# One decoder step, eight sequences of cached attention: the latent pages read a second time in 32-word pieces, transposed in blocks by VectorE, and 15 of 31 convolution taps put on GpSimd

## The chip, the core and the metric

The kernel runs on one core of a Trainium2 chip. The metric is the device time of one execution in microseconds. The kernel before took 1145.48 us (median of 3 runs, 1144.85 to 1145.82).

## The reference

One layer of a hybrid decoder, in float32, for two groups with the same weights: a prompt of 256 tokens and 8 sequences that decode one token each, against 2048 cached positions. A feed-forward half step, one projection, latent attention beside a causal depthwise convolution, a gated merge, and a second feed-forward half step. The two parts that the change touches:

```python
def absorb(carry, kv_blk, kr_blk, mask):                 # one page of 128 cached tokens of each sequence
    m, l, acc = carry
    k = _mla_keys(kv_blk, kr_blk, w_uk, g_k_head)        # kv_blk (128, 256) @ w_uk (256, 16*64), rope part, norm over 96
    sc = jnp.einsum('bshd,bphd->bhsp', qf, k) * scale
    ...
    acc = acc * corr[..., None] + jnp.einsum('bhsp,bpl->bhsl', p, kv_blk)
...
buf = jnp.concatenate([buf_prev, z], axis=1)             # 30 earlier rows, then z
y = conv(buf, w_dw) + b_dw                               # 31 taps per channel, 1024 channels
```

`cache_kv_latent` is (160, 128, 256) and `page_table` names the 16 pages of each sequence.

## The kernel before

All engines run hand-written programs that meet in semaphores. TensorE multiplies in float32r with each operand split in a high and a low part: `product` issues three matmuls (high x high, high x low, low x high; lines 1894 to 1896). The middle of the kernel goes through the 8 sequences, 16 pages of 128 tokens each, sequence 0 by itself, 1 to 6 in a loop and 7 at the end.

For each page, in four steps that overlap with those of the pages beside it:

- **TensorE, `turn`** (L2329): the page lies in `kv2` with the token on the partition. Two matmuls against the identity (L2342, L2343) turn it to latent-by-token into the PSUM bank 0. Every fourth page the rope rows of four pages are turned too (L2336), and a page later they are multiplied with the rope queries (L2338).
- **ScalarE, `page_hi`** (L1026) copies the turned page from PSUM to `kTH`, rounded; **VectorE, `page_lo`** (L1609) subtracts that from PSUM and leaves the rest in `kTL`.
- **TensorE, `keys`** (L2345): 18 matmuls of 320 to 384 columns against `wqH` and `wqL` give the page's keys of all heads and the scores of its sequence.
- **ScalarE, `page_sq`** copies the scores (L1035) and squares the keys (L1038); **VectorE, `page_sum`** sums the squares by head (L1614).

`kTH` and `kTL` hold two pages each, so the split of page n + 1 is made while TensorE computes page n. Between these, VectorE does the softmax of the sequence before in small steps (`norm_sums`, `inverse_norms`, `scores` with the maximum at L1673, `subtract`, `sums`) and the convolution: one block of 128 channels in a sequence, 31 taps on 128x256 (L1699 to L1703), spread over the pages by the table `TAPS`. GpSimd takes the maximum over the partitions (L676), squares the rope rows (L674), makes the convolution of the sample rows (L647 to L655) and adds up the blocks (L665). Behind page 10 (`VALUES_PAGE`) TensorE multiplies the probabilities of the sequence before with its 16 pages (L2367); each quarter releases four pages of `kv2`.

SyncE's queue issues the loads. For a page it reads the page number from `table` (L418), then issues the page (L425, 128 rows of 1 KB) and its rope rows (L428, 128 rows of 128 bytes). `kv2` holds two sequences; the loads of sequence b wait for the values of sequence b - 2 (`pg_rel`, L418 in the profile). Sequences 0 and 1 are loaded ahead, while the prompt's attention runs.

Of the kernel before, what the change touches and what calls it, by code (L numbers as in the profile page):

```python
# [83 lines left out]
VALUES_PAGE = 10  # L84
TAPS = (0, 1, 1, 0, 2, 2, 1, 2, 2, 2, 7, 3, 2, 3, 1, 2)
TAPS_FIRST = (2, 3, 3, 0, 2, 3, 0, 3, 3, 0, 3, 3, 0, 2, 2, 2)
# [52 lines left out]
def decoder_layer(nc, x, out):  # L139
    ctx = ExitStack()  # L140
    with ctx:
# [27 lines left out]
        vecT = sb("vecT", [P, V_N])  # L169
        gbc = sb("gbc", [P, B_N])  # L170
# [5 lines left out]
        ztmp = sb("ztmp", [P, NB, CW - 1], at=base[0] - 2112)  # L176
# [20 lines left out]
        wuvF = sb("wuvF", [P, 2, D], at=W + 16896)  # L197
        yH = sb("yH", [P, KT, T], F32R, at=W)
# [157 lines left out]
        kv2_in = [sem(f"kv2_in{g}") for g in range(8)]  # L356
        qx_done, den_ps, mx_done, gmx_done, sub_done, p_done, lsum_done = map(
# [12 lines left out]
        six_ps, six_res = sem("six_ps"), sem("six_res")  # L370
        own_act, own_dve, own_pool = sem("own_act"), sem("own_dve"), sem("own_pool")
# [18 lines left out]
        def _(sp):  # L390
# [29 lines left out]
            def page_group(i, s, g):  # L420
                b = 2 * i + s
# [10 lines left out]
            def sample_pages(i, s):  # L432
                for g in range(4):
                    sp.wait_ge(pg_rel, 4 * (2 * i + s) + g + 1)
                    page_group(i, s, g)

            def first_pages(s, groups):

                for g in groups:
                    sp.wait_ge(sc_ps, 4 * g + 4)  # L440
                    page_group(0, s, g)
# [175 lines left out]
        def _(pool):  # L617
# [40 lines left out]
            def conv_sum(f_):  # L658

                pool.wait_ge(tap_done, f_ + 1)  # L660
                if f_ == 0:
# [5 lines left out]
            pool.wait_ge(st_sb, 4)  # L667
            sample_rows(0)
            for b in range(NB):
                pool.wait_ge(kTH_done, NPG * b + 14)  # L670
                if b >= 1:
                    pool.wait_ge(norm_sum, b)
                kr = kr2[:, b % 2, :, :]
                nc.gpsimd.tensor_tensor(krq[:, :, :], kr, kr, ALU.mult).then_inc(kr_sq, 1)  # L674
                pool.wait_ge(mx_done, b + 1)
                nc.gpsimd.partition_all_reduce(gmx[:, b % 2, :], mx[:, b % 2, :], P, bass.bass_isa.ReduceOp.max  # L676
                                               ).then_inc(gmx_done, 1)
                pool.wait_ge(p_done, b + 3)
                nc.gpsimd.tensor_copy(snew[:, b, :], Pr[0:NB, b % 2, NPG, H * (b % 2):H * (b % 2) + H]).then_inc(prn_done, 1)
                if b < NB - 1:  # L680
                    conv_sum(b)
                    sample_rows(b + 1)
            conv_sum(NB - 1)
# [22 lines left out]
        def _(act):  # L706
# [314 lines left out]
            def page_hi(pg, n):  # L1021
                act.wait_ge(kT_ps, pg + 1)
                act.wait_ge(kn_ps, pg + 1)
                if n % 4 == 0:
                    f(krT[:, (n // 4) % 2, :], PS[:, 0, KL:KL + P], ACT.Copy)
                f(kTH[:, n % 2, :], PS[:, 0, 0:KL], ACT.Copy).then_inc(kTH_done, 1)  # L1026
# [25 lines left out]
            def sequence(b, s, first=False, last=False):  # L1052
                for n in range(NPG):
                    pg = NPG * b + n
                    if not (last and n == NPG - 1):
                        page_hi(pg + 1, (n + 1) % NPG)
# [10 lines left out]
            page_hi(0, 0)  # L1067
# [94 lines left out]
        def _(dve):  # L1162
# [436 lines left out]
            def page_lo(pg, n, b, s, first):  # L1599
# [3 lines left out]
                if n % 4 == 1:  # L1603
                    own.wait()
# [4 lines left out]
                v.tensor_tensor(kTL[:, n % 2, :], PS[:, 0, 0:KL], kTH[:, n % 2, :].bitcast(F32), ALU.subtract  # L1609
                                ).then_inc(kTL_done, 1)  # L1610
# [27 lines left out]
            page_lo(0, 0, 0, 0, True)  # L1638
# [895 lines left out]
```

## Time and profile before

| | |
|---|---|
| runs, us | 1145.82, 1144.85, 1145.48 (median 1145.48) |
| profiled execution, us | 1145.37, of it span 1143.5 |
| TensorE clock granted, mean | 0.997 |
| busy: TensorE, VectorE, ScalarE, GpSimd | 98%, 68%, 51%, 6% |
| DMA, mean over the span | 149 GB/s |

The span runs from the first to the last instruction of the profiled execution; the 1.9 us that its time is longer lie outside. Matmuls are pipelined, so that a busy TensorE is one that always has a matmul in its array; what a matmul costs is the distance from its start to the next one's. The mean busy shares hide the stages: the pages of the sequences lie between about 400 and 815 us of the span.

### The profile page before, as it was taken

To read this page: it belongs to the slowest core of one execution; us is meant where nothing else is said; L and a number is where in the kernel's file an instruction comes from. 1 tells how busy PE (TensorE), PEld (TensorE's weight loads), DVE (VectorE), ACT (ScalarE), POOL (GpSimd) and SP (SyncE) were. 2 spreads that over 40 slices of the span, in tenths; PEclk is the share of its full clock that TensorE was granted. 3 is DMA by queue.
4 is the path that set the end of the run, shared out by engine and by line. 5 is a ranking of instruction groups with operands and counts; after the bars stand their busy time and mean duration, and the time that the engine had idled before them with its cause. 6 is when DMAs were issued, how large, how long until landed. Compare 5 with 4: busy or idle time off the path is not lost.

```text
span 1143.5 us, 25908 instructions
## 1 busy us (share of the span) xinstructions
PE 1122.7 (98%) x9549; PEld 1086.8 (95%) x9549; DVE 778.4 (68%) x1325; ACT 581.7 (51%) x1153; POOL 67.8 (6%) x136
## 2 busy tenths in 40 slices
PE   5999999999999999999999999999999999999998
PEld 3899999999898899999999999999999999999998
DVE  4655553567777688888888888888757666555543
ACT  3444453346576655455545454554566545444432
POOL 2000000010000100101010110101020010000000
PEclk9999999999999999999999999999999999999999
DMA  9987578947344440021211202032257684555552
GB/s 324 314 292 269 183 254 289 348 167 222 99 142 127 133 133 2 20 65 33 52 47 36 62 22 73 13 84 71 57 150 254 227 272 131 183 183 177 177 184 71
DMA packets 165629, 169.84 MB, mean 149 GB/s; under 512 B 25780, under 2 KB 144071, under 8 KB 165525
## 3 DMA queue, kind: packets, MB, share of 16 engines
q1 hardware_dynamic: 163799, 166.83, 45.6%
q10 hardware_dynamic: 1742, 1.88, 0.5%
q8 instruction: 50, 0.82, 0.3%
q14 instruction: 38, 0.31, 0.1%
HBM read 167.13 MB, written 2.49 MB: 148 GB/s over the span
## 4 chain that ended last, share of the span: by engine, by line
PE 92%; DVE 2%; SPq 2%; ACT 1%; DMA 1%; issue 1%; POOL 0%; DVEq 0%; ACTq 0%
PE PS L1894 27%; PE PS L1895 27%; PE PS L1896 27%; PE PS L1971 2%; SPq L451 2%; PE PS L2367 1%; PE PS L2342 1%; PE PS L2343 1%; DMA raw<-in_w_ffn_in 1%; PE PS L2288 1%; PE PS L2099 1%; PE PS L2308 0%; PE PS L2338 0%; DVE wL L1172 0%; PE PS L2287 0%
## 5 line engine op out<-in xcount | busy, mean ns | idle before, releaser
L1172 DVE TENSOR_TENSOR wL<-raw,wH 128x1024 fp32r<-128x1024 f32 (+2 forms) x208 | 246.3, 1191 | 209.8 <-ACT wH L717 208.4
L717 ACT ACTIVATE wH<-raw 128x1024 fp32r<-128x1024 f32 (+2 forms) x208 | 213.2, 1029 | 245.6 <-PE PS L1896 224.7
L1894 PE MATMUL PS<-uH,wH 128*128 128x264 f32 x1024 | 294.2, 287 | 4.5 <-DVE uL L1233 4.0
L1895 PE MATMUL PS<-uL,wH 128*128 128x264 f32 x1024 | 291.8, 285 | 0.0
L1896 PE MATMUL PS<-uH,wL 128*128 128x264 f32 x1024 | 291.4, 285 | 0.0
L1894 PE MATMUL PS<-wqH,kTH 128*128 128x336 f32 (+2 forms) x768 | 255.7, 333 | 0.0
L1896 PE MATMUL PS<-wqH,kTL 128*128 128x336 f32 (+2 forms) x768 | 246.1, 320 | 0.0
L1895 PE MATMUL PS<-wqL,kTH 128*128 128x336 f32 (+2 forms) x768 | 245.9, 320 | 0.0
L1894 PEld LDWEIGHTS PS<-uH,wH 128*128 128x128 f32 x1024 | 193.9, 189 | 7.9 <-issue 6.4
L1895 PEld LDWEIGHTS PS<-uL,wH 128*128 128x128 f32 x1024 | 194.2, 190 | 0.0
L1896 PEld LDWEIGHTS PS<-uH,wL 128*128 128x128 f32 x1024 | 193.6, 189 | 0.0
L1614 DVE TENSOR_REDUCE nsum<-sqb 128x16 f32<-128x1024 f32 x128 | 155.0, 1211 | 1.1 <-ACT sqb L1038 1.1
L1895 PEld LDWEIGHTS PS<-wqL,kTH 128*128 128x128 f32 x768 | 144.6, 188 | 0.0
L1894 PEld LDWEIGHTS PS<-wqH,kTH 128*128 128x128 f32 x768 | 144.4, 188 | 0.0
L1896 PEld LDWEIGHTS PS<-wqH,kTL 128*128 128x128 f32 x768 | 144.2, 188 | 0.0
L1038 ACT ACTIVATE sqb<-PS 128x640 f32<-128x640 f32 (+1 forms) x256 | 138.6, 599 | 0.0
L1035 ACT ACTIVATE S<-PS 128x16 f32<-128x16 f32 x128 | 23.2, 182 | 192.0 <-PE PS L1896 192.0
L1701 DVE SCALAR_TENSOR_TENSOR u<-zbuf,wdw,u (+1 forms) x232 | 113.9, 491 | 8.2 <-DVE u L1701 7.6
L1894 PE MATMUL PS<-aH,wH 128*128 128x264 f32 x352 | 100.6, 286 | 0.0
L1895 PE MATMUL PS<-aL,wH 128*128 128x264 f32 x352 | 100.2, 285 | 0.0
L1896 PE MATMUL PS<-aH,wL 128*128 128x264 f32 x352 | 99.9, 284 | 0.0
L1609 DVE TENSOR_TENSOR kTL<-PS,kTH 128x256 fp32r<-128x256 f32 x128 | 53.8, 421 | 42.4 <-ACT kTH L1026 41.9
(343 smaller groups left out, 1497.8 us busy)
## 6 DMA issues: line engine op xcount, KB each, us to landing
raw<-in_w_ffn_in SPq DMA_DIRECT2D x86, 512.0 KB, 3.5
adaw<-in_w_ada SPq DMA_DIRECT2D x72, 512.0 KB, 6.5
raw<-in_w_ffn_out SPq DMA_DIRECT2D x32, 512.0 KB, 3.5
raw<-in_w_in SPq DMA_DIRECT2D x32, 512.0 KB, 4.5
kv<-in_cache_kv_latent SPq DMA_DIRECT2D x128, 128.0 KB, 2.0
raw<-in_w_ffn_out SPq DMA_DIRECT2D x16, 384.0 KB, 3.0
raw<-in_w_attn_out SPq DMA_DIRECT2D x8, 512.0 KB, 4.1
raw<-in_w_conv_out SPq DMA_DIRECT2D x8, 512.0 KB, 4.7
```

The lines of the kernel that those rows point to most:

```text
L451: sp.dma_start(adaw[slot][:, 2 * c:2 * c + 2, :], ada_v[:, 2 * c:2 * c + 2, ADA_W * j:ADA_W * j + ADA_W]).then_inc(ada_in[2 * slot + c // ...
L717: f(wH[:, k, 0:width], raw[:, k, 0:width], ACT.Copy).then_inc(w_hi, 1)
L1035: f(S[:, s, n, :], PS[:, b0 + bank, c:c + H], ACT.Copy)
L1038: i_ = f(sqb[:, n % 2, at:at + (k1 - k0) * w].rearrange("p (k w) -> p k w", w=w), PS[:, b0 + k0:b0 + k1, c:c + w], ACT.Square)
L1172: v.tensor_tensor(wL[:, k, 0:width], raw[:, k, 0:width], wH[:, k, 0:width].bitcast(F32), ALU.subtract).then_inc(w_lo, 1)
L1609: v.tensor_tensor(kTL[:, n % 2, :], PS[:, 0, 0:KL], kTH[:, n % 2, :].bitcast(F32), ALU.subtract).then_inc(kTL_done, 1)
L1614: v.tensor_reduce(nsum[:, s, n, :], sqb[:, n % 2, :].rearrange("p (h d) -> p h d", h=H), AX_X, ALU.add).then_inc(knsum_done, 1)
L1701: own.done(v.scalar_tensor_tensor(out=y, in0=z, scalar=w, in1=y, op0=ALU.mult, op1=ALU.add))
L1894: mm(dst, a[0], b[0], start=start, stop=False)
L1895: mm(dst, a[0], b[1], start=False, stop=False)
L1896: return mm(dst, a[1], b[0], start=False, stop=stop)
L1971: i_ = mm(PS[QUAD * g:QUAD * g + NS, bank, 0:P], csil[:, kt, :], w[:, g, :, :], start=(kt == 0), stop=(kt == KT - 1))
```

## The change

Pages of sequences 1 to 7 are no longer turned by TensorE. Each is read from HBM a second time, into a new buffer `kx` of eight pages, in an order in which a transposition of 32x32 blocks gives the page with the latent word on the partition. VectorE does that transposition (`page_turn`, one instruction of 128x256 a page, two pages ahead), from `kx` to `kT32`. ScalarE and VectorE then split the page out of `kT32`, in SBUF, through the view `BLOCKS` that puts the tokens in their order. Sequence 0 is turned as before. The loads of sequences 1 to 7 are written out in place of a loop, groups of four `kx` pages between groups of `kv2` pages.

GpSimd takes 15 of the 31 taps, each as a product (into `yp` or `ytmp`) and, but for the first, an addition; VectorE keeps 16. The maximum over partitions, the copy of the new probabilities and the squares of the rope rows stand between parts of these taps in GpSimd's program. The values of the sequence before come behind page 8 in place of 10.

```diff
-VALUES_PAGE = 10
-TAPS = (0, 1, 1, 0, 2, 2, 1, 2, 2, 2, 7, 3, 2, 3, 1, 2)
+VALUES_PAGE = 8
+TAPS = (0, 0, 0, 0, 1, 1, 0, 1, 3, 1, 1, 2, 2, 2, 1, 1)
+DVE_TAPS = sum(TAPS)
+POOL_TAPS = (DVE_TAPS, DVE_TAPS + 5, DVE_TAPS + 9, DVE_TAPS + 12, CW)
...
+        kx = sb("kx", [P, 8, KL], at=W + 16896)
+        kT32 = sb("kT32", [P, 2, KL], at=gains)
...
+        BLOCKS = [kT32[:, e, :].rearrange("p (k h t) -> p h t k", k=4, h=2) for e in range(2)]
...
+            def block_group(b, g):
+                for k in range(4):
+                    pg = page(NPG * b + 4 * g + k)
+                    src = x["cache_kv_latent"][ds(pg, 1), :, :].rearrange(
+                        "o (t k) (h q i) -> q (o t k h) i", t=QUAD, q=4, i=QUAD)
+                    sp.dma_start(kx[:, 4 * (g % 2) + k, :], src
+                                 ).then_inc(kx_in[g % 2], 16)
+            def blocks_next(b, g):
+                sp.wait_ge(kx_ps, NPG * b + 4 * g - 20)
+                block_group(b, g)
+            def pages_next(b, s, g):
+                sp.wait_ge(pg_rel, 4 * b + g + 1)
+                page_group(b, s, g)
+            def sequence_loads(b):
+                s = b % 2
+                blocks_next(b, 2)
+                blocks_next(b, 3)
+                pages_next(b + 1, 1 - s, 0)
+                blocks_next(b + 1, 0)
+                pages_next(b + 1, 1 - s, 1)
+                blocks_next(b + 1, 1)
+                pages_next(b + 1, 1 - s, 2)
+                pages_next(b + 1, 1 - s, 3)
...
+            block_group(1, 0)
+            block_group(1, 1)
+            for b in range(1, NB - 1):
+                sequence_loads(b)
+            blocks_next(NB - 1, 2)
+            blocks_next(NB - 1, 3)
+            sp.wait_ge(kx_ps, PAGES - NPG)
             sp.dma_start(wuvF[:, :, :], uv).then_inc(in_wuv, 16)
-            with sp.Fori(1, 4) as i:
-                sample_pages(i, 0)
-                sample_pages(i, 1)
...
+            def taps(f_, part):
+                for t in range(POOL_TAPS[part], POOL_TAPS[part + 1]):
+                    z, w = zbuf[:, f_, t:t + SEQ], wdw[:, f_, t:t + 1].to_broadcast([P, SEQ])
+                    own.wait()
+                    if t == DVE_TAPS:
+                        own.done(g.tensor_tensor(yp[:, :], z, w, ALU.mult))
+                    else:
+                        own.done(g.tensor_tensor(ytmp[:, :], z, w, ALU.mult))
+                        own.wait()
+                        own.done(g.tensor_tensor(yp[:, :], yp[:, :], ytmp[:, :], ALU.add))
...
+            def page_turn(b, n):
+                if n % 4 == 0:
+                    dve.wait_ge(kx_in[n // 4 % 2], 128 * b + 64 * (n // 8) - 64)
+                dve.wait_ge(kTL_done, NPG * b + n + 1)
+                v.transpose(kT32[:, n % 2, :], kx[:, n % 8, :]).then_inc(kx_ps, 1)
...
+                    v.tensor_tensor(lo_.rearrange("p (h t k) -> p h t k", h=2, k=4), BLOCKS[n % 2],
+                                    hi_.rearrange("p (h t k) -> p h t k", h=2, k=4), ALU.subtract
+                                    ).then_inc(kTL_done, 1)
...
+                if turned:
+                    tr(PS[:, 0, 0:128], kv2[:, NPG * s + n, 0:128], ident)
+                    tr(PS[:, 0, 128:256], kv2[:, NPG * s + n, 128:256], ident).then_inc(kT_ps, 1)
```

How the order moves, at two places. First SyncE's queue in the loads of a sequence (`table` holds the page numbers, `kv_...` and `kr_...` are `kv2` and `kr2`). Before, one page in the loop:

```order
L418 ISA
L418 TENSOR_LOAD table
L418 ISA x2
L425 ISA
L425 DMA kv_122<-in_cache_kv_latent 128x256
L428 ISA
L428 DMA kr_110<-in_cache_k_rope 128x32
```

Now, where a group of `kx` pages ends and one of `kv2` pages begins:

```order
L429 TENSOR_LOAD table
L429 ISA x2
L448 ISA
L448 DMA kx<-in_cache_kv_latent 128x8x32
L429 TENSOR_LOAD table
L429 ISA x2
L435 ISA
L435 DMA kv_126<-in_cache_kv_latent 128x256
L438 ISA
L438 DMA kr_114<-in_cache_k_rope 128x32
```

Every page of sequences 1 to 7 has gained a read of the table and a transfer whose rows are cut into 8 pieces of 32 words, in the one queue that also brings the pages and the rope rows.

Second VectorE, at the third page of a sequence in the loop. Before:

```order
L1609 TENSOR_TENSOR kTL<-PS,kTH 128x256
L129 REGISTER_ALU
L1701 ISA
L1701 SCALAR_TENSOR_TENSOR u<-zbuf,wdw,u 128x256
L1614 TENSOR_REDUCE nsum<-sqb 128x16
L1666 RECIPROCAL nsum<-nsum 128x128
```

Now (`kT_86` is `kT32`):

```order
L1691 STREAM_TRANSPOSE kT_86<-kx 128x256
L1708 TENSOR_TENSOR kTL<-kT_86,kTH 128x256
L1714 TENSOR_REDUCE nsum<-sqb 128x16
L1766 RECIPROCAL nsum<-nsum 128x128
```

The transposition of the page after next stands ahead of the subtraction of the next page, and the subtraction reads two tensors in SBUF; the tap is gone from this page.

## Rows read from the trace of the kernel before

**Rows 1.** The page: busy time by engine; tenths busy in 40 slices; granted clock.

```profile
PE 1122.7 (98%) x9549; PEld 1086.8 (95%) x9549; DVE 778.4 (68%) x1325; ACT 581.7 (51%) x1153; POOL 67.8 (6%) x136
...
PE   5999999999999999999999999999999999999998
PEclk9999999999999999999999999999999999999999
```

**Rows 2.** Chain that ended last, 456.4 to 771.2 us: shares by line.

```profile
by line: PE PS L1896 27.8%; PE PS L1895 27.7%; PE PS L1894 27.7%; PE PS L2367 3.6%; PE PS L2342 3.5%; PE PS L2343 3.2%; issue 2.0%; PE PS L2338 1.2%; PE PS L2336 1.0%; ACT sqb L1038 0.5%; DVE kTL L1609 0.3%; DVE olrow L1690 0.3%; DVE u L170
```

**Rows 3.** VectorE's timeline: start us, us, line, op; score maximum of two sequences.

```profile
456.37 0.64 DVE L1673 TENSOR_REDUCE mx<-S 128x16 f32<-128x272 f32 x1
...
771.17 0.64 DVE L1673 TENSOR_REDUCE mx<-S 128x16 f32<-128x272 f32 x1
```

**Rows 4.** Busy us of PE, PEld, DVE, ACT, POOL; PEclk; DMA share; GB/s.

```profile
456.40:771.20 314.80, 314.45 (x2198) 305.51 (x2197) 263.20 (x484) 162.81 (x433) 32.15 (x72) 1.00 0.17 46
```

**Rows 5.** VectorE by line, same stretch: count, busy us, mean ns, idle.

```profile
L1701 DVE SCALAR_TENSOR_TENSOR u<-zbuf,wdw,u x174 | 85.2, 490 | 7.6 <-DVE u L1701 7.6
L1609 DVE TENSOR_TENSOR kTL<-PS,kTH 128x256 fp32r<-128x256 f32 x96 | 40.4, 421 | 26.8 <-ACT kTH L1026 26.5
```

**Rows 6.** VectorE's block transposition: count, min/median/max ns.

```profile
L1240 DVE STREAM_TRANSPOSE modt<-PS x18: 307/310/319, 22.3 to 950.3; 128x128 f32<-128x128 f32 x18
```

**Rows 7.** Timeline of VectorE, then of GpSimd, at the same moments.

```profile
526.03 0.48 DVE L1701 SCALAR_TENSOR_TENSOR u<-zbuf,wdw,u  x1
526.42 1.21 DVE L1614 TENSOR_REDUCE nsum<-sqb 128x16 f32<-128x1024 f32 x1
...
527.55 0.62 DVE L1701 SCALAR_TENSOR_TENSOR u<-zbuf,wdw,u  x1
...
525.44 0.75 POOL L665 TENSOR_TENSOR ysum<-ysum,u 128x264 f32<-128x264 f32 x1 [7.45 <-issue]
...
527.45 1.81 POOL L653 TENSOR_TENSOR ztmp<-ztmp 128x120 f32<-128x120 f32 x5
```

**Rows 8.** One line each, min/median/max ns: GpSimd additions of 128x264; VectorE's taps.

```profile
L625 POOL TENSOR_TENSOR u<-u x15: 738/747/1704, 10.6 to 931.5; 128x264 f32<-128x264 f32 x15
...
L1701 DVE SCALAR_TENSOR_TENSOR u<-zbuf,wdw,u x232: 465/477/1004, 395.1 to 808.3; - x87, 128x256 f32<-128x256 f32 x29
```

**Rows 9.** SyncE's queue, timeline: start us, us, line, transfer.

```profile
554.57 0.34 SPq L425 DMA_DIRECT2D kv<-in_cache_kv_latent  x1
555.09 0.33 SPq L428 DMA_DIRECT2D kr<-in_cache_k_rope  x1
556.25 0.34 SPq L425 DMA_DIRECT2D kv<-in_cache_kv_latent  x1
```

**Rows 10.** SyncE's waits, same stretch: us in total, times, longest.

```profile
SPq L418 <- PE PS L2367: 175.2, 6, 54.3
```

**Rows 11.** DMA, 657.51 to 658.76 us: one page's rope rows.

```profile
DMA packets 145, 0.02 MB, mean 13 GB/s; under 512 B 145, under 2 KB 145, under 8 KB 145
## 3 DMA queue, kind: packets, MB, share of 16 engines
q1 hardware_dynamic: 145, 0.02, 8.7%
```

**Rows 12.** DMA, 456.4 to 771.2 us, the same columns.

```profile
q1 hardware_dynamic: 27671, 14.19, 16.9%
```

**Rows 13.** DMA, 102.4 to 107.5 us: tenths busy and GB/s in 40 slices.

```profile
DMA  9999000000000000630999255555555540022149
GB/s 835 2574 514 498 0 0 0 0 0 0 0 0 0 0 0 0 32 24 8 466 1405 1887 88 177 193 193 193 193 193 193 193 193 145 8 0 8 8 16 121 305
```

**Rows 14.** SyncE's queue at the start, 8 issues merged; then the whole line.

```profile
2.70 6.14 SPq L451 DMA_DIRECT2D adaw<-in_w_ada  x8
...
L451 SPq DMA_DIRECT2D adaw<-in_w_ada x72: 367/507/2492, 2.7 to 917.0; - x72
```

**Rows 15.** DMA, 0 to 8.84 us: packets, MB, share.

```profile
q1 hardware_dynamic: 872, 2.02, 67.6%
```

More of the change, by code:

```diff
@@ L356, in decoder_layer @@
         kv2_in = [sem(f"kv2_in{g}") for g in range(8)]
+        kx_ps, kr_ps = sem("kx_ps"), sem("kr_ps")
+        kx_in = [sem(f"kx_in{g}") for g in range(2)]
         qx_done, den_ps, mx_done, gmx_done, sub_done, p_done, lsum_done = map(
@@ L660, in conv_sum @@
                 pool.wait_ge(tap_done, f_ + 1)
+                own.wait()
+                own.done(g.tensor_tensor(u[:, f_, 0:SEQ], u[:, f_, 0:SEQ], yp[:, :], ALU.add))
+                own.wait()
                 if f_ == 0:
@@ L677, in _, with new_probabilities @@
                                                ).then_inc(gmx_done, 1)
+            def new_probabilities(b):
                 pool.wait_ge(p_done, b + 3)
-                nc.gpsimd.tensor_copy(snew[:, b, :], Pr[0:NB, b % 2, NPG, H * (b % 2):H * (b % 2) + H]).then_inc(prn_done, 1)
+                nc.gpsimd.tensor_copy(snew[:, b, :], Pr[0:NB, b % 2, NPG, H * (b % 2):H * (b % 2) + H]
+                                      ).then_inc(prn_done, 1)
+            pool.wait_ge(st_sb, 4)
+            sample_rows(0)
+            for b in range(NB):
+                taps(b, 0)
+                if b >= 1:
+                    score_max(b - 1)
+                taps(b, 1)
+                if b >= 1:
+                    new_probabilities(b - 1)
+                taps(b, 2)
+                rope_square(b)
+                taps(b, 3)
                 if b < NB - 1:
@@ L682, in _ @@
                     sample_rows(b + 1)
+            score_max(NB - 1)
+            new_probabilities(NB - 1)
             conv_sum(NB - 1)
@@ L1054, in sequence @@
                     pg = NPG * b + n
-                    if not (last and n == NPG - 1):
-                        page_hi(pg + 1, (n + 1) % NPG)
+                    if n + 1 < NPG:
+                        page_hi(b, n + 1, first)
+                    elif not last:
+                        page_hi(b + 1, 0)
                     if n == 1 and not first:
@@ L1709, in sequence @@
                     pg = NPG * b + n
+                    if n + 2 < NPG:
+                        if not first:
+                            page_turn(b, n + 2)
+                    elif not last:
+                        page_turn(b + 1, n + 2 - NPG)
                     if not (last and n == NPG - 1):
-                        page_lo(pg + 1, (n + 1) % NPG, b, s, first)
+                        page_lo(pg + 1, (n + 1) % NPG, b, s, first, first and n + 1 < NPG)
                     taps = (TAPS_FIRST if first else TAPS)[n]
@@ L1749, in _ @@
             with dve.Fori(0, 3) as i:
-                own.loop(i, 2 * (CW + 10))
+                own.loop(i, 2 * (DVE_TAPS + 10))
                 sequence(2 * i + 1, 1)
@@ L2327, in denominator, with turn @@
                 mm(PS[:, 0, 448:448 + H], ones[:, :], lsum[:, s, :], start=True, stop=True).then_inc(den_ps, 1)
-            def turn(use, s, n, pg, b, first):
+            def turn(use, s, n, pg, b, first, turned=False):
                 if n % 4 == 0:
@@ L2375, in sequence @@
                     if n + 1 < NPG:
-                        turn(use, s, n + 1, pg + 1, b, first)
+                        turn(use, s, n + 1, pg + 1, b, first, first)
                     elif not last:
@@ L2403, in _ @@
                     pe.wait_ge(masked, H)
-                    turn(0, 0, 0, 0, 0, True)
+                    turn(0, 0, 0, 0, 0, True, True)
             values(H - 1)
```

62 lines of the change are left out of this document (36 added, 26 removed).

## Prediction

> **What bounds the kernel now.** I read the page first: TensorE is busy in 98% of the span, at 9 tenths in every slice but the first and the last, with the granted clock at its 2.4 GHz level [rows 1]. So time can only be gained where TensorE has less to do, and lost wherever something makes it wait. Then the stretch that the change touches. The maximum of the scores comes once in a sequence, and from the first to the seventh 314.80 us pass [rows 3]: 52.47 us a sequence, 3.28 us a page. In it TensorE is busy for 314.45 us and VectorE for 263.20, GpSimd for 32.15 [rows 4]. The chain of waits says the same by line: the key matmuls have 83%, and the two transpositions that the change takes away have 3.5% and 3.2% [rows 2]. Last I read the SyncE queue and the DMA, which are no bound today: the queue waits 175.2 us of the stretch for pages to be released [rows 10], and its transfers take 16.9% of the 16 engines [rows 12].
>
> **TensorE: removed.** 6.7% of 314.80 us is 21.1 us for 96 pages, 0.220 us a page. The change removes it for 112 pages: 24.6 us. If all else keeps pace, a sequence falls from 52.47 to 48.95 us, a page to 3.06. The added semaphore increments and the move of the values from page 10 to 8 cost TensorE nothing: its work is the same, only two pages earlier.
>
> **VectorE: hidden.** It goes from 31 taps to 16 in a sequence. A tap lasts 0.490 us [rows 5], but overlaps its successor; 526.03 to 526.42, where the next operation starts, is some 0.40, so 15 taps are 6.0 us, and the 7.6 us of waits between dependent taps [rows 5], 1.3 a sequence, mostly go with the row of seven. A transposition of 128x128 takes 0.310 us [rows 6]; the 128 further columns can cost nothing (lower end) or the same again (0.62, upper end). I take 0.44, 0.36 after overlap, near the 0.421 of the subtraction with the same 256 columns [rows 5]: 5.8 us for 16. VectorE's 43.9 busy us (263.20 / 6) so end at 43 to 44, under 48.95. The subtraction of the low part now reads two SBUF tensors in place of PSUM and SBUF; I price it as before, at 0.42, and ScalarE's copy too.
>
> **GpSimd: hidden, if its operations leave VectorE alone.** 29 operations on 128x256; the nearest row is 0.75 us for 128x264 [rows 7], so 21.8 us, beside 5.4 that it has (32.15 / 6). It fits in 48.95, at the upper end too if not every operation takes the 1.70 us maximum [rows 8]. The cover is thin; see the third rival.
>
> **SyncE and the DMA: here I put the loss.** A `kx` page is 128 KB in 1024 pieces of 128 bytes. The rope rows are such pieces: in a window with one page's 128 pieces and 17 semaphore writes, 145 packets take 8.7% of 16 engines in 1.25 us, 1.74 us or 12.0 ns each [rows 11]. What decides is on how many engines the 1024 pieces go. When the queue copies the conv state of the samples (line 415), 8 rows in 16 pieces of 59 KB, the pieces start in two turns, slices 1 to 4 and 20 to 22 (a piece is counted whole in the slice where it starts), and behind the second turn a weight load gets a steady 193 GB/s at 5 tenths, half of the engines [rows 13]: 8 rows were dealt to 8 engines, though there were 16 pieces. The source of a `kx` page has 4 outer rows (the `q` of the rearranged pattern), the destination 128; if the deal goes by what divides both, the page goes on 4 engines, 256 pieces each: 256 x 12.0 = 3.07 us a page. The Trainium skill, DMA: Bandwidth & Descriptors, section "Why a DMA increments its semaphore by 16 and not by 1", says so outright: the engines used are the largest number up to 16 that divides the slowest dimension of both patterns, which here is 4. The trace agrees for 8 rows; no transfer in it has different outer dimensions on its two sides.
>
> Those four engines carry their share of the pages too: 16.9% of 314.80 us is 53.2 us per engine for 96 pages, 0.55 us a page. Worse, the queue is held. At the start of the kernel the eighth load in a row is out only at 8.84 us, and a single issue lasts up to 2.49 us where the median is 0.51 [rows 14]. By 8.84 us about 2450 pieces were issued (8 x 256 of these loads, 400 before) and 872 had begun [rows 15]: an estimate of 100 pieces per engine is what fits ahead. A `kx` transfer has 256 on each of its four, so SyncE stands on it until 156 are gone, and what is behind it in the queue, the table read, the pages and rope rows of the next sequence, stands too. For such a page SyncE needs 1.68 us (554.57 to 556.25) [rows 9], while the four engines need 0.55 of that.
>
> The sum for one round of `sequence_loads` (16 `kx` pages, 16 pages): 16 x 3.07 = 49.2, and 16 x 1.68 = 26.9, less what still runs on the engines when the queue changes from `kx` to pages, three times 100 x 12.0 ns = 3.6: 72.5 us, against 48.95 of TensorE. VectorE waits in `page_turn`, TensorE behind it for `kTL`. Six rounds are 435.0; the last eight `kx` pages 24.6. Ahead of the first round some 4.5 us of sequence 1 pass (its first eight pages are loaded in sequence 0, and the first buffer is free at its second page), and behind the last group 2 us to land and four pages at 3.06: 14. Together 478 us from the start of sequence 1 to the end of 7, where 7 x 52.47 = 367 are spent now. That is +111 us. The profiled execution has 1145.37 us (span 1143.5 and 1.9 around it), 0.1 under the median: I forecast **1256 us**. The weights that are loaded behind the pages come no later relative to their use than by two pages, and I give them nothing.
>
> Bounds of this case: if the queue can run ahead without limit, a page costs the four engines 3.07 + 0.55 = 3.62 us, a round 57.9, the whole 391: +23, 1169 us. If a piece that is one of eight in a strided row takes 16 ns in place of 12 (a third more; no row shows it), the round is 65.6 + 26.9 - 4.8 = 87.7, the whole 577: +210, 1355 us.
>
> **Rivals.**
> - *All 16 engines carry `kx`* (the deal goes by the 128 rows of the destination). Then a page costs 0.77 us of each engine, SyncE 1.16 us (an issue and the table read, 555.09 to 556.25 [rows 9]) beside 1.68: 2.84 us a page against 3.06. It just fits, and the 24.6 us are gained: **1121 us**. For it: nothing in the trace contradicts; a row of 128 partitions always used all engines. Against it: rows 13.
> - *16 engines, and GpSimd in VectorE's way.* A tap beside GpSimd's additions lasts 0.62 us in place of 0.48 [rows 7], one 1.00 us, and an addition up to 1.70 in place of 0.75 [rows 8]. VectorE now has 32 operations a sequence with two SBUF inputs, and GpSimd is busy 27 us of 49: each meets it with 0.56 and waits half an operation, 0.21 us, 6.7 us a sequence. VectorE comes to 51, above TensorE: seven sequences give back 7 x 2 = 14 us: **1135 us**. The Trainium skill, SBUF — State Buffer, section "Who interferes with whom", has VectorE's second read port shared with GpSimd, whoever is first keeping it for the whole instruction; the lengthened rows agree. It speaks against this change, most for the subtraction, whose second SBUF input is new.
> - *The pieces are covered after all*: four engines, but 9 ns or less a piece and no holding; the round is about TensorE's own time, and the gain of 24.6 us is eaten by late groups: within 0.2% of before.
>
> **How the numbers follow.** Four engines and a loss: 0.70. Sixteen engines: 0.25, of it 0.14 clean and 0.11 with VectorE in the way. Covered: 0.05. A measurement of this kernel can tell about 0.2%, 2.3 us, from no change. So faster 0.25, same 0.05, slower 0.70. The likeliest case alone has 1169 to 1355. The range for 8 in 10 must reach into the faster cases, which hold more than 2 in 10: 1121 to 1310, leaving out the dearest pieces and a little below.
>
> **What would show it.** Right: VectorE's transposition of every fourth page waits several us for `kx`; the issues of `kx` last 2 us or more each; DMA stands near 2 or 3 tenths and never above in the stretch; two score maxima are some 72 us apart; TensorE's busy share in the stretch is about two thirds, its clock possibly lower in the gaps. Wrong: issues of 0.35 to 0.5 us and a full DMA burst of under 1 us a page would mean 16 engines; then two maxima 49 us apart give the first rival, 51 us with taps of 0.6 us and more the second. If the issues are short but VectorE still waits for `kx`, the holding was wrong and the lower bound holds.

## The result and the profile after

The changed kernel takes 1252.91 us, the median of 4 runs (1250.25 to 1255.57), where the kernel before has 1145.58 in the same comparison: a ratio of 1.0938, 95% interval 1.0912 to 1.0964. The profiled execution, the longest of the four, has 1255.57 us with a span of 1253.7. Line numbers from here on are those of the changed kernel: the table read is L429, the page's transfer L435, its rope rows L438, the `kx` transfer L448, the block transposition L1691, the subtraction `kTL` L1708, ScalarE's copy `kTH` L1110, a tap L1801.

First the score maxima in VectorE's timeline (start us, us, line, op), beside [rows 3]:

```profile
584.86 0.62 DVE L1773 TENSOR_REDUCE mx<-S 128x16 f32<-128x272 f32 x1
...
655.83 0.63 DVE L1773 TENSOR_REDUCE mx<-S 128x16 f32<-128x272 f32 x1
...
726.91 0.62 DVE L1773 TENSOR_REDUCE mx<-S 128x16 f32<-128x272 f32 x1
```

They are 70.97 and 71.08 us apart, where [rows 3] give 52.47 a sequence. From the first maximum to the last (of sequence 7) 468.3 us pass, against 359.9 before: that is 108.4 of the 110.2 us by which the two profiled executions differ. Nearly the whole loss lies in this stretch, most of it in the five middle rounds, 513.3 to 868.6 us. The busy times of the first row below are to be read beside [rows 4], which cover six sequences; the second row is one round.

```profile
513.30:868.60 355.30, 275.29 (x1671) 260.09 (x1670) 230.84 (x409) 159.00 (x360) 130.39 (x210) 0.88 0.32 63
...
655.80:726.90 71.10, 55.52 (x335) 52.32 (x335) 46.25 (x82) 31.91 (x72) 25.98 (x42) 0.88 0.32 63
```

No engine is a bound any more: TensorE is busy for 77% of the stretch and VectorE for 65%. Who makes them wait stands in the waits of 456 to 880 us (engine, tiles, line, releaser: us in total, times, longest):

```profile
DVE kT L1691 <- DMA kx<-in_cache_kv_latent: 87.9, 17, 10.5
POOL krq L728 <- PE PS L2441: 84.9, 5, 17.8
PE PS L2441 <- DVE kTL L1708: 84.2, 17, 10.1
```

VectorE's transposition waits for a `kx` group 17 times, about 5 us each, and TensorE, in the same 17 places, for the subtraction behind it. The longest gap of a round also costs clock. In the round of the second row TensorE is idle from 665.9 to 675.1 us. Behind that gap it works at 1.2 GHz (granted clock 0.50), 18 matmuls in 5 us, where later in the round it runs 32 in 5 us at 2.4 GHz:

```profile
675.00:680.00 5.00, 4.86 (x18) 4.86 (x19) 4.64 (x10) 0.81 (x2) 0.00 (x0) 0.50 0.33 53
690.00:695.00 5.00, 4.90 (x32) 4.54 (x30) 3.69 (x6) 2.78 (x9) 2.80 (x4) 1.00 0.26 61
```

The queue's timeline for this round (start us, us, line, transfer):

```profile
660.79 0.33 SPq L438 DMA_DIRECT2D kr<-in_cache_k_rope  x1
661.90 17.93 SPq L448 DMA_DIRECT2D kx<-in_cache_kv_latent  x8
685.41 0.34 SPq L435 DMA_DIRECT2D kv<-in_cache_kv_latent  x1
...
691.89 8.31 SPq L448 DMA_DIRECT2D kx<-in_cache_kv_latent  x4
701.46 1.78 SPq L435 DMA_DIRECT2D kv<-in_cache_kv_latent  x1
...
709.39 8.35 SPq L448 DMA_DIRECT2D kx<-in_cache_kv_latent  x4
719.00 1.23 SPq L435 DMA_DIRECT2D kv<-in_cache_kv_latent  x1
```

Eight `kx` transfers, a wait to 685.41 for the values of the sequence before (L2473), four pages, four `kx`, four pages, four `kx`, eight pages. The first `kv` behind a `kx` group is held: 1.78 and 1.23 us in place of 0.34. How the engines move `kx` shows in the DMA view of 670 to 683 us, tenths busy and GB/s in 40 slices:

```profile
DMA  3333333333233333332333333223333333333333
GB/s 54 55 52 52 54 54 55 54 54 53 44 51 55 54 55 54 55 51 46 55 54 55 54 54 54 45 47 54 54 54 54 55 53 54 55 54 55 54 55 54
DMA packets 5420, 0.69 MB, mean 53 GB/s; under 512 B 5420, under 2 KB 5420, under 8 KB 5420
## 3 DMA queue, kind: packets, MB, share of 16 engines
q1 hardware_dynamic: 5420, 0.69, 33.8%
```

Never above 3 tenths and never at rest. In a microsecond without a semaphore write 424 pieces of 128 bytes start, 54 GB/s. The trace records four semaphore writes for each page (it records eight in e5 below, and sixteen for each transfer in e3). On 4 engines, which the experiments below confirm, that is 106 for one, or 9.4 ns a piece, and 256 / 106 = **2.42 us a page**. With the dips at the semaphore writes it is a little more: the seven `kx` issues listed below, from 663.8 to 678.7 us, start 2.48 us apart in the mean. The durations of the pieces overlap: 33.8% of 16 engines for 13 us and 5420 packets is 13.0 ns each. SyncE's table reads and `kx` issues between 663 and 680 us (count: min/median/max ns):

```profile
L429 SPq TENSOR_LOAD <-table x6: 728/730/740, 665.0 to 677.5; - x6
...
L448 SPq DMA_DIRECT2D kx<-in_cache_kv_latent x7: 1121/1186/1348, 663.8 to 678.7; - x7
```

Last the operations that I had priced (count: min/median/max ns; the transposition over 513.3 to 868.6 us, the two others over the whole kernel), and GpSimd's by line over that stretch (count | busy us, mean ns | idle):

```profile
L1708 DVE TENSOR_TENSOR kTL<-kT,kTH x112: 545/605/1105, 441.5 to 914.9; 128x256 fp32r<-128x256 f32 x112
...
L1110 ACT ACTIVATE kTH<-kT x112: 640/684/702, 440.7 to 914.2; 128x256 fp32r<-128x256 f32 x112
...
L1691 DVE STREAM_TRANSPOSE kT<-kx x80: 382/436/448, 513.9 to 866.2; 128x256 f32<-128x256 f32 x80
```

```profile
L720 POOL TENSOR_TENSOR yp<-yp,ytmp 128x256 f32<-128x256 f32 x70 | 52.1, 745 | 5.5
L718 POOL TENSOR_TENSOR ytmp<-zbuf,wdw 128x256 f32<-128x256 f32 x70 | 43.8, 626 | 41.2 <-issue 36.9
```

### The profile page after: what moved, and what is told of

Same layout as the page of the kernel before. It is cut to its first block, busy times and chain, and to the rows that moved or that the text cites. A ratio compares the mean times of both kernels' runs of the same rounds, so it can differ in the third digit from the quotient of the medians.

```text
span 1253.7 us, 26235 instructions
## 1 busy us (share of the span) xinstructions
PE 1138.8 (91%) x9325; PEld 1091.6 (87%) x9325; DVE 792.3 (63%) x1317; ACT 614.1 (49%) x1153; POOL 235.5 (19%) x376
## 4 chain that ended last, share of the span: by engine, by line
PE 65%; SPq 20%; issue 5%; DMA 5%; DVE 3%; ACT 2%; POOL 0%; DVEq 0%; ACTq 0%
PE PS L1999 19%; PE PS L2000 19%; PE PS L2001 19%; SPq L429 8%; SPq L448 6%; SPq L435 3%; DMA kx<-in_cache_kv_latent 3%; SPq L438 3%; PE PS L2076 2%; DMA adaw<-in_w_ada 1%; PE PS L2473 1%; DVE kTL L1708 1%; PE PS L2393 0%; PE PS L2204 0%; PE PS L2441 0%
## 5 line engine op out<-in xcount | busy, mean ns | idle before, releaser
L1999 PE MATMUL PS<-wqH,kTH 128*128 128x336 f32 (+2 forms) x768 | 264.6, 345 | 0.8 <-DVE kTL L1708 0.7
L2000 PE MATMUL PS<-wqL,kTH 128*128 128x336 f32 (+2 forms) x768 | 256.9, 334 | 0.0
L2001 PE MATMUL PS<-wqH,kTL 128*128 128x336 f32 (+2 forms) x768 | 256.5, 334 | 0.0
L1999 PEld LDWEIGHTS PS<-wqH,kTH 128*128 128x128 f32 x768 | 153.9, 200 | 5.0 <-DVE kTL L1708 2.3
L2000 PEld LDWEIGHTS PS<-wqL,kTH 128*128 128x128 f32 x768 | 153.9, 200 | 0.0
L2001 PEld LDWEIGHTS PS<-wqH,kTL 128*128 128x128 f32 x768 | 153.4, 200 | 0.0
L1691 DVE STREAM_TRANSPOSE kT<-kx 128x256 f32<-128x256 f32 x112 | 48.5, 433 | 99.2 <-DMA kx<-in_cache_kv_latent 97.2
L2441 PE MATMUL PS<-const,kr 128*128 128x128 f32 x32 | 11.3, 354 | 93.7 <-DVE kTL L1708 93.7
```

What stands on the lines that cost most here:

```text
L1691: v.transpose(kT32[:, n % 2, :], kx[:, n % 8, :]).then_inc(kx_ps, 1)
L1999: mm(dst, a[0], b[0], start=start, stop=False)
L2000: mm(dst, a[0], b[1], start=False, stop=False)
L2001: return mm(dst, a[1], b[0], start=False, stop=stop)
```

## The experiments

Two questions were open. First, why `kx` is late: too few engines, or something that any 1024 pieces would meet. Second, what would be left of the 24.6 us that TensorE saves if `kx` came in time.

### e1_plain: whole rows in place of pieces

```diff
-                    src = x["cache_kv_latent"][ds(pg, 1), :, :].rearrange(
-                        "o (t k) (h q i) -> q (o t k h) i", t=QUAD, q=4, i=QUAD)
+                    src = x["cache_kv_latent"][ds(pg, 1), :, :].rearrange("o p n -> p (o n)")
```

> The second read is made of whole 1 KB rows (128 rows, 128 pieces, so 16 engines); kx then holds the page untransposed by chunk, so the keys are of another arrangement of the page: the reordering is what this kernel leaves out. All other instructions stay. Theory A (the 1024 pieces sit on 4 engines and SyncE's queue stands behind them): the stall goes, SyncE needs about 1.62 + 1.1 us a page against TensorE's 3.06, and the time is 1121 to 1135 us. Theory C (the work moved to VectorE, ScalarE and GpSimd is what costs): the time stays over 1200 us.

1139.47 us, ratio 0.9951 (0.9934 to 0.9968): nearer to theory A than to C, but above the 1121 to 1135 us of A. The sequences take 50.8 to 52.4 us. With the transfer out of the way the change does gain, but some 6 us, not 24.6. The three lines that matter, 513 to 820 us, and ScalarE's copy in the kernel before over the same stretch:

```profile
L1109 ACT ACTIVATE kTH<-kT 128x256 fp32r<-128x256 f32 x88 | 60.6, 689 | 0.0
L1707 DVE TENSOR_TENSOR kTL<-kT,kTH 128x256 fp32r<-128x256 f32 x89 | 58.7, 660 | 14.2 <-ACT kTH L1109 13.4 <-issue 0.3
...
L1800 DVE SCALAR_TENSOR_TENSOR u<-zbuf,wdw,u (+1 forms) x83 | 52.9, 637 | 0.9 <-DVE u L1800 0.9
```

```profile
L1026 ACT ACTIVATE kTH<-PS 128x256 fp32r<-128x256 f32 x89 | 36.0, 405 | 0.0
```

All three are longer than in the kernel before ([rows 5] for VectorE): the copy 0.69 us (0.405 before), the subtraction 0.66 (0.421), a tap 0.64 (0.490). VectorE is busy for 282.5 of 307 us. What lengthens them is the question of e6 to e8.

### e2_p16: the same 1024 pieces, 16 outer rows

```diff
-                    src = x["cache_kv_latent"][ds(pg, 1), :, :].rearrange(
-                        "o (t k) (h q i) -> q (o t k h) i", t=QUAD, q=4, i=QUAD)
+                    src = x["cache_kv_latent"][ds(pg, 1), :, :].rearrange("o p n -> (o p n)").rearrange(
+                        "(b a i) -> a b i", a=16, i=QUAD)
```

> The same 1024 pieces of 128 bytes a page, but the source pattern has 16 outer rows in place of 4 (another order of the pieces: the arrangement of the page is what this kernel leaves out). Theory A: 16 engines carry 64 pieces each, 0.6 us a page, and the time is that of the kernel with whole rows, within 10 us. Theory B (the queue hands out some 424 pieces per us whatever the engines, which is the rate in the trace of the change): 2.4 us a page remain and the time stays within 15 us of 1253.

1151.16 us, ratio 1.0046 (1.0029 to 1.0062). The count and the size of the pieces are those of the change, only the outer dimension is 16 in place of 4, and about 102 of the 107 us are gone. Against e1 11.7 us remain, a little more than the 10 that theory A allowed: VectorE still waits 14.1 us for `kx` between 513 and 820 us, and SyncE's own work fills the round: 16 x (1.32 + 1.61) and 5.3 of waiting for the values are 52.2 us, where e1's sequences take 50.8 to 52.4. A `kx` issue lasts 0.56 us. DMA, 587 to 593 us:

```profile
DMA  0289996000079997200399994100699982387684
GB/s 0 33 129 200 218 190 98 7 0 0 16 127 169 208 207 107 40 0 0 62 152 197 212 161 71 19 0 0 106 181 203 212 136 36 68 177 212 219 215 81
```

Bursts of 9 tenths and over 200 GB/s, with pauses between: all engines work. So theory B, a limit on handing out pieces that is the same whatever the outer dimension, is ruled out.

### e3_four: the right order, in four transfers of 32 rows

```diff
-                        "o (t k) (h q i) -> q (o t k h) i", t=QUAD, q=4, i=QUAD)
-                    sp.dma_start(kx[:, 4 * (g % 2) + k, :], src
-                                 ).then_inc(kx_in[g % 2], 16)
+                        "o (t k) (h q i) -> q t (o k h) i", t=QUAD, q=4, i=QUAD)
+                    for q in range(4):
+                        sp.dma_start(kx[QUAD * q:QUAD * q + QUAD, 4 * (g % 2) + k, :].rearrange("t (c i) -> t c i", i=QUAD),
+                                     src[q]).then_inc(kx_in[g % 2], 16)
...
-                    dve.wait_ge(kx_in[n // 4 % 2], 128 * b + 64 * (n // 8) - 64)
+                    dve.wait_ge(kx_in[n // 4 % 2], 512 * b + 256 * (n // 8) - 256)
```

> The right order, each page by four transfers of 32 rows, which go on 16 engines. The transfer of a page falls from 2.4 to 0.6 us, but SyncE issues four where it issued one: one table read of 0.73 us and four issues of 0.38 to 0.52, so 2.3 to 2.8 us a page beside 1.62 for the other loads. If SyncE's own time is the next bound, a round takes 62 to 71 us and the kernel 1200 to 1255 us. If only the engines' time mattered, it would be 1121 to 1140 us.

1344.9 us, ratio 1.174 (1.172 to 1.176): much slower than the change, and outside both expectations. SyncE's timeline from 636.65 and its issues in the same place tell why:

```profile
636.65 15.29 SPq L449 DMA_DIRECT2D kx<-in_cache_kv_latent  x17
...
L449 SPq DMA_DIRECT2D kx<-in_cache_kv_latent x18: 563/564/587, 635.9 to 651.4; - x18
L429 SPq TENSOR_LOAD <-table x5: 268/277/284, 637.3 to 652.0; - x5
```

17 transfers take SyncE 15.29 us. It starts one every 0.75 us (0.56 for the issue, 0.18 between), and the next page's first 1.32 us after the last: 3 x 0.75 + 1.32 = 3.57 us a page, whatever the engines do. 16 x 3.57 + 26 = 83 us, and the middle sequences take 84.2 to 85.2. So the time is not a matter of engines alone: SyncE is a bound of its own. The DMA view of 637 to 650 us shows what the engines do with the pieces in their right order (GB/s in 40 slices):

```profile
GB/s 13 88 0 78 23 0 0 68 33 41 60 8 86 8 97 4 0 0 58 43 50 51 6 92 2 49 52 0 0 77 24 32 69 1 123 2 0 69 32 0
```

Zeros between bursts of up to 123 GB/s, twice the rate that `kx` has in the change: it is not the order of the pieces that holds the change at 54 GB/s.

### e5_p8: eight outer rows

```diff
+                    src = x["cache_kv_latent"][ds(pg, 1), :, :].rearrange("o p n -> (o p n)").rearrange(
+                        "(b a i) -> a b i", a=8, i=QUAD)
```

> The same 1024 pieces a page, but the source pattern has 8 outer rows instead of 4; the order within the page is left out. Theory A (the pieces are dealt to as many engines as the outer dimension allows): 8 engines, 128 pieces each, 9.4 ns a piece, so 1.20 us a page; a round of 16 pages and 16 kx pages is 16 x 1.20 + 26 + about 5 = 50 us, close to VectorE's 51 to 53, so 1150 to 1175 us, with VectorE waiting 15 to 45 us for kx. Rival (what mattered in the run with 16 rows was another order of the pieces, not the number of engines): time jumps with the order, either near 1151 or near 1253.

1204.34 us (two runs), ratio 1.0513 (1.0494 to 1.0532); the middle rounds take 61.8 to 63.5 us. Neither expectation holds for the time. DMA, 580 to 590 us, and SyncE beside it:

```profile
DMA  6666200566661015666500266663003566640066
GB/s 103 103 109 109 40 0 0 81 110 108 110 98 17 0 19 92 109 109 109 84 3 0 42 108 110 108 109 48 0 0 55 81 109 108 109 62 1 6 97 109
```

```profile
L429 SPq TENSOR_LOAD <-table x5: 725/727/728, 581.1 to 588.8; - x5
...
L448 SPq DMA_DIRECT2D kx<-in_cache_kv_latent x6: 679/680/687, 580.3 to 590.0; - x6
```

Eight engines do what they should: 109 GB/s, twice the 55 of four, so 1.2 us a page. The rate goes with the outer rows, not in a jump with the order of the pieces. But a page comes only every 1.93 us, and between two the engines rest (the zeros). SyncE needs 0.68 for the issue, 0.73 for the next table read and 0.52 for the register work between. 16 x 1.93 + 26 + 5.4 of waiting for the values is 62.3. In e2 the same table read takes 0.275 us and a page 1.32:

```profile
L429 SPq TENSOR_LOAD <-table x3: 267/275/283, 587.8 to 590.5; - x3
```

### e12_p8_one_read: the same, with one table read for four `kx` pages

```diff
+                pg = page(NPG * b + 4 * g)
                 for k in range(4):
-                    pg = page(NPG * b + 4 * g + k)
```

> As e5 (8 outer rows, 8 engines), but SyncE reads the page table once for a group of four kx pages instead of once for each; the four transfers of a group all fetch the group's first page (the other three pages are left out). The bytes, pieces and engines are those of e5. In e5 SyncE starts a kx transfer every 1.93 us, while its pieces take the engines about 1.2 us, so that they stand idle in between. Theory (in e5 SyncE's own time is the bound, not the engines): transfers of a group start 0.9 to 1.2 us apart, a round falls from 62.4 to about 52 to 54 us, the time to 1150 to 1165 us. Rival (eight engines themselves are too slow): 1204 us as e5.

1161.41 us, ratio 1.0147 (1.0120 to 1.0173), as the theory had it. The rounds take 53.1 and 55.1 to 55.9 us, in turn. SyncE, 587 to 593 us:

```profile
587.32 4.36 SPq L448 DMA_DIRECT2D kx<-in_cache_kv_latent  x4
...
L448 SPq DMA_DIRECT2D kx<-in_cache_kv_latent x4: 679/925/1148, 587.3 to 590.9; - x4
```

Four transfers go out in 4.36 us, and now their issues do lengthen, because the engines are behind. The same bytes, pieces and engines as in e5, and 43 us less: there SyncE was the bound. With e2, e3 and e5 this gives the rule of a round. A `kx` page costs the larger of two times: the engines' 2.42, 1.2 or 0.6 us (4, 8 or 16 of them), and SyncE's own 1.9, 1.9, 1.3 us, or 3.6 in e3. In the change the engines are above SyncE by only 0.5 us a page.

### e6_taps: only the taps are moved

Every page is turned by TensorE as before, there is no `kx`; the tables of taps, `POOL_TAPS` and page 8 for the values are those of the change.

```diff
-                        page_hi(b, n + 1, first)
+                        page_hi(b, n + 1, True)
...
-                        turn(use, s, n + 1, pg + 1, b, first, first)
+                        turn(use, s, n + 1, pg + 1, b, first, True)
```

> No kx at all: every page turned by TensorE as before, only the 15 taps on GpSimd and the tables of taps as in the change. If GpSimd's operations cost TensorE nothing: 1145 us, same as before, VectorE's taps 0.5 us. If GpSimd in VectorE's way costs by itself: 1150 or more, taps and subtraction 0.6 us. If the freed VectorE helps: 1140 to 1144.

1144.55 us, ratio 0.9993 (0.9984 to 1.0002): no difference that can be told, as in the first of the three expectations, though the taps are not at its 0.5 us. 513 to 820 us:

```profile
L1790 DVE SCALAR_TENSOR_TENSOR u<-zbuf,wdw,u (+1 forms) x83 | 46.6, 561 | 0.9 <-DVE u L1790 0.9
L1695 DVE TENSOR_TENSOR kTL<-PS,kTH 128x256 fp32r<-128x256 f32 x89 | 37.4, 421 | 49.4 <-ACT kTH L1097 49.4
```

A tap, with two inputs in SBUF, is lengthened to 0.561 us; the subtraction, which still has one input in PSUM, stays at 0.421 to the nanosecond. VectorE is busy for 227 us in place of 257, and TensorE, always busy, gets nothing from that.

### e7_plain_few and e8_plain_flat: what lengthens the copy and the subtraction

e7 is e1 without 14 of GpSimd's 15 taps; e8 is e1 with the block order read straight through.

```diff
-POOL_TAPS = (DVE_TAPS, DVE_TAPS + 5, DVE_TAPS + 9, DVE_TAPS + 12, CW)
+POOL_TAPS = (DVE_TAPS, DVE_TAPS + 1, DVE_TAPS + 1, DVE_TAPS + 1, DVE_TAPS + 1)
```

```diff
-        BLOCKS = [kT32[:, e, :].rearrange("p (k h t) -> p h t k", k=4, h=2) for e in range(2)]
+        BLOCKS = [kT32[:, e, :].rearrange("p (h t k) -> p h t k", k=4, h=2) for e in range(2)]
```

> The kx pages as whole rows (as in e1), and 14 of the 15 taps on GpSimd left out (the convolution is wrong by them). Theory: GpSimd's operations lengthen VectorE's with two SBUF inputs, and that ate the gain of the removed transpositions: VectorE's subtraction falls from 660 to 450 ns, taps from 630 to 490, TensorE's waits for kTL end, sequence 49 to 50 us, 1122 to 1130 us. Rival (the strided reading of the block order is what lengthens the subtraction and the copy): both stay above 600 ns and the time stays at 1135 to 1140 us.

> The kx pages as whole rows, all taps as in the change, but the subtraction and ScalarE's copy read the transposed page in plain order instead of with a stride (the order of the words is left out). Theory (GpSimd): subtraction stays near 0.6 us, ScalarE's copy falls from 0.68 to 0.4 us, time 1134 to 1139 us. Rival (stride): subtraction falls to 0.42 to 0.5 us and the time to 1122 to 1130 us.

e7: 1131.2 us, ratio 0.9869 (0.9854 to 0.9884). e8: 1128.78 us, ratio 0.9855 (0.9840 to 0.9871). Of e7, 513 to 820 us, then of e8:

```profile
L1109 ACT ACTIVATE kTH<-kT 128x256 fp32r<-128x256 f32 x88 | 60.3, 686 | 0.0
L1707 DVE TENSOR_TENSOR kTL<-kT,kTH 128x256 fp32r<-128x256 f32 x89 | 54.0, 606 | 21.2 <-ACT kTH L1109 20.8 <-issue 0.3
L1800 DVE SCALAR_TENSOR_TENSOR u<-zbuf,wdw,u (+1 forms) x83 | 39.4, 475 | 0.9 <-DVE u L1800 0.9
```

```profile
L1800 DVE SCALAR_TENSOR_TENSOR u<-zbuf,wdw,u (+1 forms) x83 | 52.9, 638 | 0.9 <-DVE u L1800 0.9
L1707 DVE TENSOR_TENSOR kTL<-kT,kTH 128x256 fp32r<-128x256 f32 x88 | 46.2, 525 | 11.6 <-ACT kTH L1109 10.8 <-issue 0.3
L1109 ACT ACTIVATE kTH<-kT 128x256 fp32r<-128x256 f32 x88 | 38.0, 432 | 0.0
```

There are two causes. With 14 of GpSimd's 15 taps left out, VectorE's tap falls from 637 to 475 ns and the copy not at all (689 to 686); read straight through, the copy falls to 432 and the tap not at all. The subtraction has a part of both: 660 with both, 606 with the stride alone, 525 with GpSimd alone. I had expected GpSimd to hold all of the subtraction; that was wrong, the stride holds more of it. If the two parts (135 and 54 ns) add up, 471 ns are left where the kernel before has 421; those 50 stay open, since both together were not taken out. By time the stride is worth 10.7 us of e1 and GpSimd 8.3.

### e4_half: half of the pages through `kx`

Pages 0 to 7 of sequences 1 to 7 through `kx`, pages 8 to 15 turned by TensorE.

```diff
-                blocks_next(b, 2)
-                blocks_next(b, 3)
-                pages_next(b + 1, 1 - s, 0)
                 blocks_next(b + 1, 0)
-                pages_next(b + 1, 1 - s, 1)
                 blocks_next(b + 1, 1)
-                pages_next(b + 1, 1 - s, 2)
-                pages_next(b + 1, 1 - s, 3)
+                for g in range(4):
+                    pages_next(b + 1, 1 - s, g)
...
-                        turn(use, s, n + 1, pg + 1, b, first, first)
+                        turn(use, s, n + 1, pg + 1, b, first, first or n + 1 >= 8)
```

> Only pages 0 to 7 of sequences 1 to 7 go through kx; pages 8 to 15 are turned by TensorE as before. Theory A: SyncE and the four engines need 8 x 2.42 + 16 x 1.62 = 45 us a sequence, under TensorE's 51; half of the gain is left, 56 x 0.22 = 12 us: 1131 to 1140 us, faster than both kernels. Theory C: slower than the kernel before by what the work moved to VectorE and GpSimd costs, 1150 us or more.

1143.28 us (1140.38 to 1146.98, 10 runs), ratio 0.998 (0.997 to 0.999): faster than the kernel before by 2 us, not by the 5 to 14 of theory A. `kx` is no longer late: a round asks 8 x 2.42 + 26 = 45 us of SyncE. Yet in the profiled execution, the longest of the ten, two of the seven sequences take 54.7 us and the others at most 51.5. The waits of the first slow one, 508.6 to 563.3 us:

```profile
PEld PS L1993 <- ACT sqb L1117: 2.3, 1, 2.3
DVE kT L1685 <- issue: 2.3, 1, 2.3
PE PS L1993 <- DVE kTL L1702: 2.0, 1, 2.0
```

Once in the sequence VectorE pauses for 2.3 us before a transposition with nothing to wait for, and TensorE then stands for 2 us; its clock falls to 0.97 in this stretch. VectorE runs two sequences per trip of a loop, and the pause is where the loop goes back to its start. It does so twice, and there are two pauses. The kernel before and e1 have them too, shorter (513 to 820 us, in this order: us in total, times, longest):

```profile
DVE Srope L1605 <- issue: 3.3, 2, 1.7
DVE kT L1690 <- issue: 2.6, 2, 1.5
```

### e9, e10, e11: the loops written out

```diff
-            with dve.Fori(0, 3) as i:
-                own.loop(i, 2 * (DVE_TAPS + 10))
+            for i in range(3):
                 sequence(2 * i + 1, 1)
                 sequence(2 * i + 2, 0, i)
-                own.end(3)
```

and the same for ScalarE and TensorE: e9 from e4, e10 from e1, e11 from the kernel before.

> As e4 (pages 0 to 7 of sequences 1 to 7 through kx, 8 to 15 turned by TensorE), with the three-trip loops over two sequences on VectorE, ScalarE and TensorE written out. In e4 every second sequence takes 54.7 us instead of 51.5, with a pause of 2.3 us of VectorE before a transposition and 2 us of TensorE behind it. Theory (the pause is the loop's turn, which the longer chain of transposition, copy and subtraction can't absorb): all sequences take 51.5 us, three times 3.2 us are gained, 1134 us. Rival (the first group of kx pages lands late every second sequence): 1143 us as e4.

> As e1 (kx as whole rows, order left out), with the same loops written out. If the loop's turn costs 1 to 1.4 us every second sequence there too: 1135 to 1137 us. If not: 1139 us.

> The kernel before with the same loops written out and nothing else. Its sequences take 52.5 and 52.4 us alternately and TensorE is busy all the time, so the loop's turn is hidden: 1144 to 1146 us. If it gains more than 3 us, the loops cost both kernels alike and e9's gain is not due to kx.

e9: 1138.36 us (1138.11 to 1139.24), ratio 0.9936 (0.9920 to 0.9953). It beats both kernels, the one before by 7 us, and it leaves nothing of the work out. Its sequences take 51.4 to 51.8 us. The gain over e4 is 4.9 us where I expected 9.6. I had counted three slow sequences where there are two, and I had read their 3.2 us from the longest of e4's executions, 3.7 us above its median. TensorE is busy again, 508 to 817 us:

```profile
508.00:817.00 309.00, 307.34 (x2143) 296.51 (x2145) 256.00 (x432) 175.46 (x422) 150.00 (x235) 1.00 0.29 67
```

e10: 1138.7 us, 0.8 under e1, within the scatter of both, so there the pauses cost next to nothing. e11: 1143.97 us, ratio 0.9985 (0.9975 to 0.9995): the loops cost the kernel before 1.5 us. So of e9's 7 us some 1.5 are to be had without `kx`. VectorE's pauses are gone in all three; which of the three loops mattered was not taken apart.

## Why the prediction came out as it did

The forecast was 1256 us, measured were 1252.91; the case that I gave 0.70, four engines and a loss, is what happened. But the sum came this near by luck: two errors of its terms, of opposite sign, nearly cancel.

- **On how many engines the pieces go.** Right, and it decided everything. The same 1024 pieces cost 1253, 1204 and 1151 us with 4, 8 and 16 outer rows (1161 with 8 where SyncE has less to do), and the trace has 4 semaphore writes a page in the change. It rested on [rows 13] and on the rule that I cited. That is the Trainium skill, DMA: Bandwidth & Descriptors, section "Why a DMA increments its semaphore by 16 and not by 1": it gives 4, 8 and 16 engines for these three patterns, and the runs agree.
- **The price of a piece.** I took 12.0 ns from [rows 11]; 9.4 were measured, 2.42 us a page, not 3.07: 38.7 us a round where I had 49.2. The 12.0 ns were a duration in the record, and such durations overlap (13.0 ns recorded at a piece every 9.4). [Rows 11] could give only the duration: the rate needs a stretch in which the engine has no pause.
- **The held queue.** Right in kind, wrong in size. I said that issues of `kx` would last 2 us or more and that some 100 pieces an engine fit ahead. They last 1.19 us (0.62 for the first of a group). More fits ahead than 100: the last of the eight issues in the round shown ends at 679.83 us and its last pieces start at 683.2, so that over 300 pieces an engine were still to go at the measured rate. The estimate from [rows 14, 15] does not carry over from pieces of 2 and 4 KB to 128-byte ones.
- **The order of the terms of a round.** I took off 3.6 us for work of the engines that goes on while SyncE issues pages, and gave SyncE's wait for the values nothing. In truth the first `kv` behind a group is held (1.4 and 0.9 us too long in the round shown), and SyncE waits 23.1 us in 5 rounds for TensorE's values. Measured: 38.7 + 16 x 1.61 + 2.3 + 4.6 = 71.4 us, against 70.7 to 71.6 in the trace and 72.5 forecast. 10.5 us too much for the pieces stood against 9.4 too little for the rest, and nothing in the prediction made them alike.
- **SyncE as a bound.** Not in the sum: with `kx` it needs 1.9 us a page of its own, only 0.5 below the engines. Had the pattern had eight outer rows I would have forecast a round near 48 us; e5 measured 61.8 to 63.5.
- **TensorE.** I expected it busy for about two thirds of the stretch, with a lower clock in the gaps; it is 77% busy at a mean granted clock of 0.88 of 2.4 GHz. 275.29 us for five sequences is 55.1 each, where 52.4 less 3.5, 48.9, was its work. Its key matmuls last 0.343 us in the mean, where they last 0.324 before; over 288 in a sequence that is 5.3 of the 6.2 us, which the stretches at 1.2 GHz cost.
- **VectorE and GpSimd.** The transposition has its 0.44 us, GpSimd's operations 0.63 and 0.75, about 26 us a sequence where I had 27. The subtraction and ScalarE's copy, which I left at their old prices, were the wrong term here: 0.605 for 0.421 and 0.684 for 0.405. Behind the late `kx` it did not matter. With 16 engines it did. e2 is the case of the first two rivals, and with 1151 us it lies 30 above the first (1121, all clean) and 16 above the second (1135, VectorE above TensorE); some 12 of that is the transfer, whose pages cost SyncE 1.32 us each and not 1.16. In e1, without that, the first would have been wrong by 18 us and the second by 4, and the second for half of its reason only, since it named GpSimd and not the stride. GpSimd's own part showed where [rows 7] had it, on operations with two inputs in SBUF: taps of 637 ns with it and 475 without, and none on the subtraction from PSUM in e6. The Trainium skill, SBUF — State Buffer, section "Who interferes with whom", has it so, and the trace agrees.

The Trainium skill, SBUF — State Buffer, section "Door 1: The DMA port swizzle (why `[64,N]` ≈ `[32,N]`)", has a note by which reading at full rate wants at least two accesses within the same 16 bytes. It gives no time for an engine, but it would have warned of the stride that I left at nothing: the innermost step of the block order is 256 bytes. The measured 689 against 432 ns for ScalarE's copy agrees; the runs do not show where the threshold lies.

What stays open is why a table read takes 0.73 us behind a transfer on 4 or 8 engines and 0.27 behind one on 16. The Trainium skill, DMA: Bandwidth & Descriptors, section "Why a DMA increments its semaphore by 16 and not by 1", says that the issuing sequencer itself writes what is missing to 16 when fewer engines take part. The rows fit an additional step of that kind, but no run separates it. And a transfer with the right order and 16 outer rows was not tried, so what the change would bring with it is known only from kernels that leave the order out (e2, 1151 us).

## What to carry to other kernels

When a transfer is cut into small pieces, read first which outermost dimension its two patterns have, since it sets how many engines share the pieces; then price the page three times, by the engines' rate, by the queue's own instructions (issue, table read, register work) and by what stands behind it in the queue, and take the largest. A price for a piece needs a stretch where an engine has no pause, not a duration. And an operation whose operand moves from PSUM to a strided tile in SBUF is a new operation: price its stride and its port apart, also when it is only "the same copy".

## What the runs showed of the hardware

- Pieces of 128 bytes from memory to SBUF: one every 9.4 ns on an engine (106 a us), at 4 engines (55 GB/s) and at 8 (109 GB/s).
- The issue of a transfer costs SyncE by its pattern: 0.34 us for 128 rows of 1 KB, 0.56 for 1024 pieces on 16 engines, 0.62 on 4, 0.68 on 8; a `kx` page's table read behind it 0.27 us (16 engines) or 0.73 (4 or 8).
- Where the loop over two sequences goes back, VectorE pauses without a releaser: 1.7 us at most in the kernel before, 1.5 in e1, 2.4 in e4, and nothing with the loops written out. Writing them out gained 1.5 us, 0.8 (within the scatter) and 4.9.
- A 128x256 copy by ScalarE lasts 0.69 us where the innermost step of its input in SBUF is 256 bytes, and 0.43 where it is read straight through.
- A VectorE operation with two inputs in SBUF is longer while GpSimd works (taps of 0.48 us become 0.56 to 0.64); one with an input in PSUM stays at 0.421 us.
